# Weight pieces of a fused layer's first block reordered, with its first four projection groups computed in two halves of the contraction

## The reference, cut to what matters

```python
c_act = jax.nn.silu(c)
mod = c_act @ w_ada[l] + b_ada[l]                      # (1024) @ (1024, 6144)
sh1, sc1, ga1, sh2, sc2, ga2 = jnp.split(mod, N_MOD, axis=-1)
u = modulate(rmsnorm(h, g_norm1[l]), sh1, sc1)         # rmsnorm(h) * (1 + sc1) + sh1
y = hybrid_mixer(u, w_in[l], ...)                      # proj = u @ w_in, then conv, gated linear attention
h = h + ga1[:, None, :] * y
...                                                    # a mixture of 32 experts follows
modf = c_act @ w_ada_f + b_ada_f                       # (1024) @ (1024, 2048)
...
# in hybrid_mixer:
p_conv, q, k, v, r, a1, gates = jnp.split(u @ w_in, offs, axis=-1)
z = a * sigmoid(gt)                                    # a, gt are the halves of p_conv
z = lax.conv_general_dilated(z, w_dw, ...)             # depthwise, 31 taps
```

## Time and profile before

| | us |
|---|---|
| median of three runs | 2339.4 (2338.03 to 2341.51) |
| span of the profiled execution | 2341.2 |
| PE busy in the span | 2290.1 (98%) |
| DVE busy | 1087.2 (46%) |
| ACT busy | 422.8 (18%) |
| PE busy in the first 40 us | 21.5 |
| PE busy between 120 and 300 us | all of it |

### The profile page before, as it was taken

One profiled execution on the slowest core, in us unless ns is written; L12 is line 12 of the kernel. 1 busy time (PEld: TensorE's weight loads), 2 busy tenths in 40 slices (PEclk: granted clock), 3 DMA queues, 4 the chain that ended last, 5 costly groups with the idle time before them and its releaser, 6 DMA issues.

```text
span 2341.2 us, 28956 instructions
## 1 busy us (share of the span) xinstructions
PE 2290.1 (98%) x12084; PEld 1553.3 (66%) x12084; DVE 1087.2 (46%) x2045; ACT 422.8 (18%) x838; POOL 48.9 (2%) x77
## 2 busy tenths in 40 slices
PE   6999999999999989999999999999999999999998
PEld 4778854444444458748877768847866877676873
DVE  2788431111111166653463356666664255335675
ACT  1123321111111111100322221102100141221110
POOL 1000000000000010000000000000000000000000
PEclk9999999999999999999999999999999999999999
DMA  9656668999999965444330544527445342044541
GB/s 386 263 216 253 229 192 352 422 422 422 422 422 422 417 211 176 155 161 156 108 136 2 180 139 158 180 94 242 153 158 180 126 162 92 38 144 153 180 163 53
DMA packets 175998, 499.74 MB, mean 213 GB/s; under 512 B 6905, under 2 KB 99337, under 8 KB 146065
## 3 DMA queue, kind: packets, MB, share of 16 engines
q1 hardware_dynamic: 171920, 481.23, 54.7%
q0 software_dynamic: 3824, 16.43, 2.3%
q10 hardware_dynamic: 144, 0.52, 0.1%
HBM read 491.34 MB, written 6.82 MB: 213 GB/s over the span
## 4 chain that ended last, share of the span: by engine, by line
PE 89%; DMA 8%; DVE 1%; ACT 1%; issue 0%; SPq 0%; POOL 0%; DVEq 0%; POOLq 0%
PE bank L2123 21%; PE bank L2163 11%; PE bank L1429 7%; DMA ring<-in_w 7%; PE bank L2211 6%; PE bank L865 6%; PE bank L1466 3%; PE bank L2414 3%; PE bank L2276 2%; PE bank L2547 2%; PE bank L2101 2%; PE bank L2593 2%; PE bank L1413 2%; PE bank L2270 2%; PE bank L2517 2%; PE bank L1450 2%
## 5 line engine op out<-in xcount | busy, mean ns | idle before, releaser
L2123 PE MATMUL bank<-Tw,Sx 128*128 128x256 f32 x960 | 213.8, 379 | 0.0
L2123 PEld LDWEIGHTS bank<-Tw,Sx 128*128 128x128 f32 x960 | 179.3, 190 | 22.7
L2211 PE MATMUL bank<-xT,ring 128*128 128x256 f32 x704 | 152.6, 379 | 0.0
L865 PE MATMUL bank<-xT,ring 128*128 128x256 f32 x640 | 143.9, 385 | 2.8 <-ACT xT L283 2.8
L2211 PEld LDWEIGHTS bank<-xT,ring 128*128 128x128 f32 x704 | 133.4, 190 | 18.0
L2123 PE MATMUL bank<-ring,xT 128*128 128x256 f32 x640 | 144.7, 379 | 0.0
L865 PEld LDWEIGHTS bank<-xT,ring 128*128 128x128 f32 x640 | 122.9, 193 | 22.0 <-ACT xT L283 2.9
L2123 PEld LDWEIGHTS bank<-ring,xT 128*128 128x128 f32 x640 | 121.6, 190 | 18.2 <-issue 1.9
L1429 PE MATMUL bank<-ring,xg 128*64 128x512 f32 x512 | 113.9, 593 | 5.1 <-DMA ring<-in_w 5.1
L1466 PE MATMUL bank<-ring,hTg 128*64 128x512 f32 x512 | 113.4, 595 | 0.0
L1429 PE MATMUL bank<-more,xg 128*64 128x512 f32 x512 | 112.6, 592 | 0.0
(11 more groups left out here) (519 smaller groups left out, 3565.2 us busy)
## 6 DMA issues: line engine op xcount, KB each, us to landing
ring<-in_w SPq DMA_DIRECT2D x128, 1024.0 KB, 17.3
ring<-in_ffn_w_in SPq DMA_DIRECT2D x88, 1024.0 KB, 7.7
ring<-in_first_pieces SPq DMA_DIRECT2D x33, 2048.0 KB, 12.2
more<-in_w SPq DMA_DIRECT2D x64, 1024.0 KB, 17.1
ring<-in_ffn_w_out SPq DMA_DIRECT2D x20, 2048.0 KB, 7.8
ring<-in_w_mix_in SPq DMA_DIRECT2D x12, 2048.0 KB, 7.8
ring<-in_xattn_w_kv SPq DMA_DIRECT2D x8, 2048.0 KB, 8.1
ring<-in_w_mix_out SPq DMA_DIRECT2D x4, 2048.0 KB, 9.7
```

The lines of the kernel that those rows point to most:

```text
L865: last = nc.tensor.matmul(b[:, c * SEQ:(c + 1) * SEQ], w[:, k, m * P:(m + 1) * P], xT[:, k, :], start=(k == 0), stop=(k == KD - 1))
L2123: last = nc.tensor.matmul(bank[BANK_OF[name]][:, 0:SEQ], lhs(k), rhs(k), start=(k == 0), stop=(k == 3))
L2211: last = nc.tensor.matmul(b[:, c * SEQ:(c + 1) * SEQ], w[:, k, col:col + P], xT[:, k, :], start=(k == 0), stop=(k == KD - 1))
```

## The change

Three things are changed together.

1. The order of pieces. Pieces in 0 and in 1 (columns 0 to 1023 of w_in, all 1024 rows) are cut the other way: `head 0` holds rows 0 to 511 of those columns and `head 1` rows 512 to 1023. The new order is ada 0, ada 2, head 0, ada 1, ada 3, head 1, and then ten pairs (ada n + 4, in n + 2), then ada 14 and ada 15.
2. The start on PE, ACT and DVE. After ada 0 and ada 2 the lower half of the modulation is computed, chunks 0 to 3 of `xT` are written, and PE multiplies groups 0, 1, 2 (in two parts) and 3 with their first four chunks only (`head(g, 0)`), with the work on ada 1 and ada 3 in between. ACT and DVE meanwhile copy chunks 4 to 7 unmodulated out of their banks and modulate them in place later. Then PE adds the second half (`head(g, 1)`).
3. What follows. `ada_mm(4)` to `ada_mm(8)` move to behind groups 3, 5, 6, 8 and 12; DVE's sums 5 to 8, its takes and its taps are put in another order, with `ada_sum(8)` directly ahead of the level loop. POOL's router transfers move behind its wait for `proj_full` 1, and the rest of the constants is issued behind piece 8.

The core of the diff:

```diff
-PIECES1 = ([("ada", n) for n in range(4)] + [p for n in range(12) for p in (("in", n), ("ada", n + 4))]
+ADA_FIRST = (0, 2, 1, 3)
+PIECES1 = ([("ada", 0), ("ada", 2), ("head", 0), ("ada", 1), ("ada", 3), ("head", 1)]
+           + [p for n in range(10) for p in (("ada", n + 4), ("in", n + 2))] + [("ada", 14), ("ada", 15)]
            + [("pw", 0), ("glao", 0), ("glao", 1), ("out", 0), ("out", 1), ("kv", 0)])
...
                 if kind == "ada" and n < 4:
-                    sp.wait_ge(ada_part, n + 1)
+                    sp.wait_ge(ada_part, ADA_FIRST.index(n) + 1)
+                elif kind == "head":
+                    if n == 0:
+                        sp.wait_ge(head_half, 1)
+                    else:
+                        sp.wait_ge(proj_full, 4)
...
-                if j == SLOTS:
+                if j == 2 * SLOTS:
                     sp.dma_start(K[:, NCONST_FIRST:, :], a["const_tiles"][:, NCONST_FIRST:, :]
...
-            pool.dma_start(wr[:, :, :], a["w_router"]).then_inc(rows_loaded, 16)
-            pool.dma_start(brow[:, :], a["b_router"].partition_broadcast(P)).then_inc(rows_loaded, 16)
             st.sync()
             norm_rstd(pool, 0)
             pool.wait_ge(proj_full, 1)
+            pool.dma_start(wr[:, :, :], a["w_router"]).then_inc(rows_loaded, 16)
+            pool.dma_start(brow[:, :], a["b_router"].partition_broadcast(P)).then_inc(rows_loaded, 16)
...
             ada_partial(0)
             norm_transposes(pe, 0, 0)
+            ada_columns(0)
             ada_partial(1)
-            ada_columns(0)
+            ada_columns(1)
+            pe.wait_ge(xT_act, 1)
+            pe.wait_ge(xT_dve, 1)
+
+            def head(g, part, cs=(0, 1)):
+
+                w = slot_w(wait_piece(pe, J1["head", part]), 4, 1024)
+                for c in cs:
+                    for k in range(4):
+                        last = nc.tensor.matmul(bank[g][:, c * SEQ:(c + 1) * SEQ],
+                                                w[:, k, g * 256 + c * P:g * 256 + (c + 1) * P], xT[:, 4 * part + k, :],
+                                                start=((part, c, k) == (0, 0, 0)), stop=((part, c, k) == (1, 1, 3)))
+                return last
+
+            head(0, 0)
+            head(1, 0)
             ada_partial(2)
-            ada_columns(1)
+            head(2, 0, (0,))
             ada_partial(3)
+            head(2, 0, (1,))
             ada_columns(2)
             ada_columns(3)
-            pe.wait_ge(xT_act, 1)
-            pe.wait_ge(xT_dve, 1)
+            head(3, 0).then_inc(head_half, 1)
+            pe.wait_ge(xT_act, 2)
+            pe.wait_ge(xT_dve, 2)
...
-                if g == G_A1:
+                if g < NB:
+                    last = head(g, 1)
+                elif g == G_A1:
...
-            for i, g in enumerate((1, 3, 5, 7, 10)):
+            for i, g in enumerate((3, 5, 6, 8, 12)):
                 after[g].append(("ada", 4 + i))
...
-            dve.wait_ge(proj_dve, 2)
-            ada_sum(6)
-            convolve(6)
-            ada_sum(7)
-            for p in range(2):
-                if p:
-                    convolve(3)
...
+            dve.wait_ge(proj_dve, 2)
+            convolve(2)
+            ada_sum(5)
+            convolve(1)
+            ada_sum(6)
+            ada_take(5)
+            convolve(3)
+            keys(0)
+            ada_take(6)
+            convolve(2)
+            ada_sum(7)
+            keys(1)
...
-            ada_take(8)
-            convolve(3)
+            ada_take(7)
+            convolve(4)
...
+            ada_sum(8)
             dve.wait_ge(consts_loaded, 48)
...
-                if l > 1:
-                    ada_take(7 + l)
+                ada_take(7 + l)
```

## The result

The changed kernel takes 2363.7 us (median of four runs, 2360.66 to 2369.49) against 2339.0 for the kernel before (four runs, 2338.03 to 2341.51): a ratio of 1.0105, 95% interval 1.0087 to 1.0123, so it is slower by about 1%. Its profiled execution spans 2358.9 us, 17.7 more than the 2341.2 of before.

What follows compares the result with a forecast made beforehand. The start was taken as bound by DMA, the rest by PE. Level 0 at 118.4 against 117.91, the loop's +14.2 and 3.1 for clock put level 8 +17.8: span 2359.0, less 1.8 gives 2357.2 us (2349 to 2368).

Steps and rivals of the forecast that it cites:

- The start: Up to the fourth group: projections start at about 25.6, 3.1 us lost to clock, head start 4.4 us.
- The transfers behind it: Up to level 0: held slot delays later pieces, PE waits 4.8 us before ada_mm(6), level 0 at 118.4 against 117.91.
- my signs: Expected trace marks, among them DVE waiting for DMA before sum of ada 6 and PE for DVE before ada_mm(6).
- The level loop: Level 0 to level 8: ada pieces about 7 us late each turn bind the levels, 14.2 us in all.
- first two terms: Level loop: level 0 to 2 takes 39.5 us (+6.2), level 2 to 4 takes 37.9 us (+5.0).
- The third term: Level loop from level 4 to the end: late ada 13 costs +2.4, a tap +0.6, together +3.0 us.
- The clock: Level loop: waits may lower PE's clock; one half-clock stretch of 3.1 us on the path, bounds zero to three.
- The shift passes on whole: Behind level 8: order unchanged, so the +17.8 us reaches the end, span 2359.0 us.
- The step from the span to the median: Whole program: median of the runs taken 1.8 us below the profiled span of 2359.0, giving 2357.2.
- The surviving head start: Rival: ada pieces reach DVE in time, level loop keeps its pace, 4.4 us gain stays; 2331.9 us, chance 0.06.
- the draw: Rival: first bill as told, but late pieces cost the level loop only the last 3.0 us; 2342.9 us, chance 0.07.
- The falling clock: Rival: PE's clock falls after four more of about eight new waits, 12.4 us more; 2369.6 us, chance 0.14.

Runs made afterwards that it cites:

- e3_rows_in_gap: Changed kernel with POOL issuing the router's and bias rows' transfers after the fourth partial product instead of after group 0; 2351.4 us (1.0052).
- e5_in2_first: e4_both with in 2 ahead of ada 5 in the list of pieces instead of behind it; 2336.0 us over eleven runs (0.9987).
- e4_both: Changed kernel with ada pieces one ahead again and POOL's row transfers issued earlier, in the transfer gap; 2340.8 us (0.9998).
- e2_before_ada_late: Kernel before with only the order of pieces edited, so that ada 9 to 15 come one release later; 2352.6 us (1.0054).
- e1_ada_ahead: Changed kernel with ada 5 put ahead of in 2, so that ada pieces run one ahead again; 2345.0 us (1.0022).

## Why the prediction was right

**The start** was sized too small. In the profiled execution the transposes ended at 17.7 and not 19.1, the second piece landed at 17.0 and the projections began at 23.9 (forecast 25.6). And the 3.1 us of lowered clock did not come there: 32 rows took 7.15, nearly the full-clock 6.9. The head start was 9 us in this trace and not 4.4. That is partly the luck of the execution. The changed kernel and e3_rows_in_gap have such a start; in the other five traces with the start in two halves the projections begin at 24.0 to 25.2, the first 32 rows take 8.6 to 9.8 us, and the fourth group ends at 60.0 to 61.0, 5.5 to 6.5 us ahead of before:

```profile
24.04 9.80 PE L847 MATMUL bank<-xT,ring 128*128 128x256 f32 x32 [1.80 <-ACT xT L1049]
```

This row is of e5_in2_first. The lowered clock of the forecast is in these traces, at 1.7 to 2.9 us above the full-clock 6.9.

**The transfers behind it.** The mechanism was right. Windows of the changed kernel (same columns), in the gap behind head 1:

```profile
40.00:42.00 2.00, 2.00 (x12) 1.79 (x12) 1.31 (x6) 0.99 (x2) 0.00 (x0) 1.00 0.00 0
...
44.00:46.00 2.00, 2.00 (x11) 1.77 (x10) 0.00 (x0) 0.00 (x0) 0.00 (x0) 1.00 0.72 139
```

Nothing moves from 37 to 44 us, 7 us rather than the 12 that I had, since head 0's slot came free at 43.9 and not 48.3. ada 4 was summed from 51.5 (forecast 56.2). The step that failed is the wait for the rows. I charged them only as bytes ahead of in 3 and ada 6, and overlooked that DVE's take of ada 4, ahead of sum 5, waits for them itself. PE's wait came one `ada_mm` earlier than I said and was 10.2 us instead of 4.8. At level 0 it cost hardly more than forecast in the end, because two other terms were off the other way: ada 6 landed at 79.9 and not 82.9, so that DVE, 5.0 us late for it, reached it at 84.9, only 2.0 behind my path; and group 11 lost 1.9 us to the clock where I had 3.1. Level 0 at 118.8 against 118.4 is therefore partly luck. e3_rows_in_gap is the measurement of it: without the wait, and with the rows' bytes moved, level 0 is 6.1 us earlier. Of my signs, the wait of DVE before the sum of ada 6 and that of PE before ada_mm(6) did not show.

**The level loop** was right in mechanism and in its first two terms: 39.4 us from level 0 to 2 (forecast 39.5) and 38.1 from level 2 to 4 (37.9). The pair issued at 127.6 shows the landing on which they rest, against the earlier trace rows:

```profile
DMA to landing us min/median/max: 7.8/10.0/12.3
```

The third term was mis-sized: 69.8 us from level 4 on instead of 65.4, or 68.5 with the 3.1 us of lowered clock that I had put apart. Of the 7.4 above the 62.4 of before, a wait of 3.8 before ada_mm(13) is the sum of ada 13 (I had 2.4; its piece landed 13.8 us after its issue and not 12.5), and two half-clock stretches of 3.4 us at 196 to 200 and 227 to 230 take up to 3.4.

```profile
198.00:200.00 2.00, 2.00 (x12) 1.97 (x11) 1.67 (x3) 0.00 (x0) 0.00 (x0) 0.56 0.00 0
...
228.00:230.00 2.00, 2.00 (x5) 0.99 (x4) 2.00 (x5) 0.00 (x0) 0.00 (x0) 0.50 0.95 410
```

**The clock** fell in the loop behind ada_mm(9), at level 4 and from ada_mm(13) on, three times for about 3.4 us. I had taken one on the path at 3.1 us, with zero to three as bounds. Each costs about 1.7, and the first was absorbed, since PE waited 0.9 us behind it at level 2 all the same. So the term came out near its size with two stretches of half the price.

**The shift passes on whole** was right but for one wait behind the last level, where PE stands for DVE's take of the sum of ada 15, the last late piece:

```profile
269.39 1.13 PE L973 MATMUL bank<-v,AT 128*128 128x256 f32 x4 [1.37 <-DVE rows L1192]
```

The shift grows from 19.8 to 21.4 us there: the experts' first product starts at 382.4 instead of 360.9 and their last 21.6 later. The spans differ by only 17.7, since the kernel before ran at half clock at two later places where this execution did not. Each such stretch of 3.4 us is worth 1.7.

```profile
1220.00:1222.00 2.00, 2.00 (x24) 1.88 (x22) 0.69 (x1) 0.00 (x0) 0.00 (x0) 0.50 0.00 0
1974.00:1976.00 2.00, 2.00 (x32) 1.78 (x30) 1.10 (x2) 0.00 (x0) 0.00 (x0) 0.50 0.00 0
```

So the profiled span hit the forecast of 2359.0 to 0.1 us by luck: 2.0 us more at the last level and 1.6 behind it, less what the later stretches gave back. The median of the runs, 24.7 us above before, is 6.5 above my 2357.2 and inside the range. The step from the span to the median is where the 6.5 come from. I took the median 1.8 us below the profiled span, as it had been for the kernel before. In every execution on record that has both numbers, the time is 1.8 us above its own span (2360.7 for 2358.9 here). So the profiled execution of before, with a span of 2341.2, belongs to a time near 2343.0 (an estimate), 4.0 above its median, and the changed kernel's lies 3.0 below its own. In medians the change costs 24.7 us and not 17.7. The two longer executions of the changed kernel have spans of 2364.9 and 2367.7 and a mean granted clock of 0.987, against 0.990 and 0.991 in the two shorter ones. The same work with more time at half clock would give just these means (an estimate: 0.990 x 2358.9 / 2364.9 = 0.9875), and the five other traces of this start show one place for it, the first 32 rows. Where these executions lost it isn't recorded.

**The rivals.** The surviving head start and the draw are out by the measured time. e4_both and e5_in2_first show under which order a head start does survive, and how little of it: in e5_in2_first 6.1 us at the fourth group shrink to 1.6 at the last level. The falling clock is true in part, three stretches in the loop rather than one after every wait.

## What to carry to other kernels

When weights come through an in-order queue into a few slots, write down for every release which piece it brings in and when each consumer asks for that piece. Moving one stream one step ahead moves another one step back, and what counts is whether the lateness (here 16.5 us a turn) exceeds the room (9.6). A start that is made earlier by holding a slot longer leaves the transfer engines idle, and the bytes then come in a bunch; look also at what else waits in that bunch, small transfers of another queue included. And where executions of one kernel differ, compare a span with a span and a median with a median: one trace may show a short or a long execution of its kernel.

## What the runs showed of the hardware

A transfer that POOL issues among SP's pieces can take long. The last of the rows, 1 MB issued at 49.8, had landed 23.9 us later, while five pieces issued between 43.9 and 58.1 were on their way. In e3_rows_in_gap the same transfer, issued at 39.1 into idle transfer engines, had landed after 8.3 us, ahead of the sum of ada 4, and DVE had no wait for it. I had only counted the bytes.

The length of a wait does not tell whether the clock falls behind it. In the changed kernel it fell behind waits of 2.19 us (level 4) and 3.8 us (before ada_mm(13)), but stayed at 1.00 behind those of 0.94 (level 2) and 1.56 us (before ada_mm(11)):

```profile
160.00:162.00 2.00, 2.00 (x12) 1.77 (x11) 1.89 (x4) 0.00 (x0) 0.00 (x0) 1.00 0.00 0
...
188.00:190.00 2.00, 2.00 (x11) 1.76 (x10) 2.00 (x6) 0.00 (x0) 0.00 (x0) 1.00 1.02 434
```

In e2_before_ada_late it stayed at 1.00 behind a wait of 2.18 us at the same level 4. The kernels without a wait in the loop (e1_ada_ahead, e4_both, e5_in2_first) still show one half-clock stretch there, behind ada_mm(9), whose matmuls have one column each:

```profile
142.00:144.00 2.00, 2.00 (x7) 1.56 (x6) 2.00 (x6) 0.61 (x1) 0.00 (x0) 0.51 1.03 442
```

This row is of e5_in2_first. In the kernel before, the same products at 142.0 had no such stretch behind them. By the Trainium skill (TensorE: Matmul & The Clock Gate, HAM oscillation) waits for DMA between bursts of matmuls make the clock fall again each time. The runs agree for a long wait (0.50 behind the 6.9 us that PE waits for in 2 in e1_ada_ahead) and show that it also falls without one. What exactly decides it was not measured.
